# First MLP of a two-layer trunk on Trainium2: its shift and scale loaded by halves of columns, and no unread TensorE products ahead of it

## The reference, cut to what matters

```
sh_m, sc_m, gt_m, sh_f, sc_f, gt_f = split(silu(c) @ ada_w[i] + ada_b[i], 6)
h  = rms_norm(x, norm_g[i, 0]) * (1 + sc_m) + sh_m
x  = x + gt_m * rms_norm(mixer(h), norm_g[i, 1])
hf = rms_norm(x, norm_g[i, 2]) * (1 + sc_f) + sh_f
x  = x + gt_f * rms_norm(square(relu(hf @ ffn_w1[i])) @ ffn_w2[i], norm_g[i, 3])
```

## Time and profile before

| what | value |
|---|---|
| median of 3 runs | 944.35 us (943.44 to 946.1) |
| the profiled execution's own time | 945.35 us |
| its span in the profile | 943.6 us |
| PE busy | 923.8 us, 98% |
| DVE, ACT busy | 635.5 us (67%), 418.4 us (44%) |
| mean granted clock of PE | 0.996 of full |
| DMA moved | 165.63 MB, mean 176 GB/s |

### The profile page before, as it was taken

The page is one execution under the profiler, slowest core; times in us unless marked ns, Lnnn a source line. Parts: engine busy times, 40 slices in busy tenths (PEclk is TensorE's granted clock), DMA queues, the critical chain, the costliest instruction groups (busy, mean ns, idle before and its releaser), DMA issues.

```text
span 943.6 us, 11434 instructions
## 1 busy us (share of the span) xinstructions
PE 923.8 (98%) x4647; PEld 760.5 (81%) x4647; DVE 635.5 (67%) x624; ACT 418.4 (44%) x513; POOL 43.9 (5%) x76
## 2 busy tenths in 40 slices
PE   8889999999999999999999999999999999999997
PEld 6658877888888888889888888898888888888886
DVE  5696299489578866686667545757856964784444
ACT  6554474455246433264222224555634624643422
POOL 3002000010001001000101000000000000000000
PEclk9999999999999999999999999999999999999999
DMA  9999439617834585424656531273871561246201
GB/s 307 316 352 346 160 135 284 250 55 197 288 114 113 163 331 207 129 71 172 210 178 209 196 114 45 82 275 129 231 265 45 156 223 45 90 122 236 89 23 67
DMA packets 89036, 165.63 MB, mean 176 GB/s; under 512 B 4206, under 2 KB 34002, under 8 KB 88984
## 3 DMA queue, kind: packets, MB, share of 16 engines
q1 hardware_dynamic: 83656, 154.20, 47.6%
q0 software_dynamic: 5328, 10.70, 5.5%
HBM read 158.56 MB, written 6.32 MB: 175 GB/s over the span
## 4 chain that ended last, share of the span: by engine, by line
PE 53%; DVE 1%; issue 0%; ACT 0%; DVEq 0%
PE ps L657 18%; PE ps L658 17%; PE ps L659 17%; PE ps L751 1%; DVE y L1552 0%; DVE in_lo L1563 0%; PE ps L686 0%; ACT in_hi L1191 0%; DVE y L1558 0%; DVE xs L1928 0%; DVE y L1515 0%; DVE y L1509 0%; DVEq L136 0%; ACT work L1163 0%; DVE st L1549 0%
## 5 line engine op out<-in xcount | busy, mean ns | idle before, releaser
L657 PE MATMUL ps<-in_hi,w_parts 128*128 128x512 f32 (+1 forms) x784 | 290.0, 370 | 0.9 <-DVE in_lo L1563 0.4
L658 PE MATMUL ps<-in_lo,w_parts 128*128 128x512 f32 (+1 forms) x784 | 288.1, 367 | 0.0
L659 PE MATMUL ps<-in_hi,w_parts 128*128 128x512 f32 (+1 forms) x784 | 288.1, 367 | 0.0
L1389 DVE TENSOR_TENSOR w_parts<-raw,w_parts 128x2048 fp32r<-128x2048 f32 x81 | 185.5, 2291 | 140.2 <-ACT w_parts L1085 140.1
L1085 ACT ACTIVATE w_parts<-raw 128x2048 fp32r<-128x2048 f32 x81 | 154.8, 1911 | 223.7 <-PE ps L659 204.2
L657 PEld LDWEIGHTS ps<-in_hi,w_parts 128*128 128x128 f32 x784 | 147.8, 188 | 29.4 <-issue 3.3
L659 PEld LDWEIGHTS ps<-in_hi,w_parts 128*128 128x128 f32 x784 | 147.8, 188 | 24.4
L658 PEld LDWEIGHTS ps<-in_lo,w_parts 128*128 128x128 f32 x784 | 147.8, 189 | 24.1
L657 PE MATMUL ps<-w_parts,ops_hi 128*128 128x512 f32 x240 | 93.8, 391 | 2.3 <-DVE y L1441 0.9
L658 PE MATMUL ps<-w_parts,ops_hi 128*128 128x512 f32 x240 | 93.4, 389 | 0.0
L657 PE MATMUL ps<-w_parts,mid_hi 128*128 128x512 f32 x192 | 75.0, 391 | 0.0
(11 more groups left out here) (192 smaller groups left out, 1044.8 us busy)
## 6 DMA issues: line engine op xcount, KB each, us to landing
raw<-in_ffn_w_dram SPq DMA_DIRECT2D x58, 1024.0 KB, 5.4
ada_raw<-in_ada_w_dram SPq DMA_DIRECT2D x56, 512.0 KB, 6.2
xs<-in_ffn_w_dram SPq DMA_DIRECT2D x12, 1024.0 KB, 5.6
raw<-in_conv_in_w_dram SPq DMA_DIRECT2D x16, 512.0 KB, 5.2
xs<-in_ffn_w_dram POOLq DMA_DIRECT2D x6, 1024.0 KB, 8.7
raw<-in_ada_w_dram SPq DMA_DIRECT2D x4, 1024.0 KB, 11.0
ada_sum<-in_ada_w_dram SPq DMA_DIRECT2D x4, 1024.0 KB, 12.8
win<-in_ada_w_dram SPq DMA_DIRECT2D x4, 1024.0 KB, 12.1
```

The costliest lines, as they stand in the source:

```text
L657: nc.tensor.matmul(o, hi, b_hi, start=start, stop=False, skip_group_check=on)
L658: nc.tensor.matmul(o, hi, b_lo, start=False, stop=False, skip_group_check=on)
L659: return nc.tensor.matmul(o, lo, b_hi, start=False, stop=stop, skip_group_check=on)
L1389: nc.vector.tensor_tensor(w_lo[:, u % W_SLOTS, :], raw_of(u), w_hi[:, u % W_SLOTS, :].bitcast(F32), ALU.subtract).then_inc(w_lo_ready, 1)
```

## The change

Four things change, all between the mixer's end and the end of unit 4.

1. The eight late pieces are cut another way. A piece is now 256 rows by 512 columns of shift and the same of scale; four pieces make one half of the columns (`SUMS` 8 and 9). Each is loaded by two DMAs of 512 KB with contiguous runs of 2 KB. In `add_up` a late piece is 4 products of 512 columns in place of 8 of 256.
2. `stay_busy(0, 6)` goes, and the four `turn_up` of the late sums become two `turn_late` (4 small products each). ACT's `copy_late` and DVE's `late_columns` handle four chunks at once.
3. All eight transposed parts go through ACT's `copy_first` to `xt`. The order is chunks 0 to 3 for all tokens, then chunks 4 to 7. Scaling, high part and low part are made chunk by chunk over all 512 tokens.
4. Unit 1 is multiplied chunk by chunk over 512 tokens. PE's order is new: transposes 0 and 1, pieces 14 and 15, transposes 2 and 3 and `turn_late(0)` stand ahead of the first product. On ACT and DVE the splits of unit 3 now stand behind the high and low parts of chunks 4 to 7.

```
 PRE = (... + [(GATE_M, c) for c in range(4)]
-       + [(s, c) for c in range(4) for s in (SCALE_F, SHIFT_F)])
+       + [(h, kk) for h in range(2) for kk in range(UK)])
-SUMS = ... + [(PRE_F + 2 * c, PRE_F + 2 * c + 1) for c in range(4)]
+SUMS = ... + [tuple(PRE_F + UK * h + kk for kk in range(UK)) for h in range(2)]
@@ load_pre
+                if i >= PRE_F:
+                    h, kk = PRE[i]
+                    rows = ada_rows(0)[:, 2 * kk:2 * kk + 2, SHIFT_F * D:(SCALE_F + 1) * D].rearrange("p k (s n) -> p k s n", s=2)
+                    for s in range(2):
+                        sp.dma_start(pre_slot(i)[:, :, s, :], rows[:, :, s, half(h)]).then_inc(pre_in[PRE_SLOTS[i]], 16)
@@ add_up
+                if i >= PRE_F:
+                    for j in range(4):
+                        mm = nc.tensor.matmul(ps[32 * j:32 * (j + 1), sums_bank(n), :], silu_wide[:, 1, 2 * PRE[i][1] + j % 2, :], pre_slot(i)[:, j % 2, j // 2, :],
+                                              start=first, stop=last)
+            def turn_late(h):
+                pe.wait_ge(late_picks, 1)
+                pe.wait_ge(ada_row, cols_value(8 + h))
+                for j in range(4):
+                    mm = nc.tensor.matmul(ps[:, sums_bank(8 + h), 2 * j:2 * j + 2], late_row[:, h, j * P:(j + 1) * P], pick_late[:, :], start=True, stop=True)
@@ PE, ahead of ffn(0)
             add_up(PRE_F)
             add_up(PRE_F + 1)
-            stay_busy(0, 6)
-            turn_up(8)
+            turn_first(0)
+            turn_first(1)
+            add_up(PRE_F + 2)
+            add_up(PRE_F + 3)
+            turn_first(2)
+            turn_first(3)
+            turn_late(0)
@@ start_pairs, new (the old one is in the listing above)
+                need_weights(1)
+                chunk(1, 0)
+                turn_first(4)
+                turn_first(5)
+                chunk(1, 1)
+                add_up(PRE_F + 4)
+                turn_first(6)
+                turn_first(7)
+                chunk(1, 2)
+                add_up(PRE_F + 5)
+                chunk(1, 3).then_inc(unit_done, 1)
+                need_weights(2)
+                pe.wait_ge(xt_copied, len(FIRST_TURNED))
+                add_up(PRE_F + 6)
+                second_unit(2)
+                add_up(PRE_F + 7)
+                second_unit(3)
+                turn_late(1)
+                second_unit(0)
+                pe.wait_ge(cols_read, cols_value(9))
+                second_unit(1).then_inc(unit_done, 1)
+                for u in (3, 4):
+                    need_weights(u)
+                    for m in range(4):
+                        for k in range(UK):
+                            if m == 0:
+                                pe.wait_ge(f_lo, UK + k + 1)
+                            last = feat_products(u, k, m, u - 3, UK + k, COLS, ALL, False, k == UK - 1)
+                        last.then_inc(bank_done, 1)
@@ ACT, new order after first_root(0), first_root(1)
             first_root(2)
             first_root(3)
+            copy_first(0) ... copy_first(3)
+            copy_late(0)
+            for n in range(4):
+                first_hi(n)
+            copy_first(4)
+            copy_first(5)
             split_hi(2)
+            copy_first(6)
+            copy_first(7)
+            copy_late(1)
+            for n in range(4, 8):
+                first_hi(n)
             split_hi(3)
@@ DVE, new order after first_norm(0), first_norm(1)
             first_x(3)
             first_norm(2)
             first_norm(3)
+            late_columns(0)
+            first_input(0), (1), first_lo(0), first_input(2), first_lo(1), first_input(3), first_lo(2), (3)
             split_lo(2)
+            late_columns(1)
+            first_input(4), (5), first_lo(4), first_input(6), first_lo(5), first_input(7), first_lo(6), (7)
             split_lo(3)
```

More of the change, by code:

```diff
@@ L282, in pre_slot @@
                     win[:, 0:4, :].rearrange("p a t -> p (a t)"), win[:, 4:8, :].rearrange("p a t -> p (a t)"))[PRE_SLOTS[i]]
-            return slot.rearrange("p (k n) -> p k n", k=NC)
+            return slot.rearrange("p (k s n) -> p k s n", k=2, s=2) if i >= PRE_F else slot.rearrange("p (k n) -> p k n", k=NC)
         def pre_value(i):
-            return 16 * PRE_SLOTS[:i + 1].count(PRE_SLOTS[i])
+            return sum(32 if b >= PRE_F else 16 for b in range(i + 1) if PRE_SLOTS[b] == PRE_SLOTS[i])
         def sums_of(i):
@@ L941, in start_pairs, with chunk @@
             def start_pairs():
[L944 to L950, removed]
-                    return last
[L953 to L960, removed]
+                def chunk(u, k):
+                    pe.wait_ge(f_lo, k + 1)
+                    for m in range(4):
+                        last = feat_products(u, k, m, u - 1, k, COLS, ALL, k == 0, False)
+                    return last
                 def second_unit(m):
-                    need_weights(2)
                     for k in range(UK):
@@ L1807, in first_lo, with late_columns @@
-            def first_lo(i):
-                dve.wait_ge(f_hi, i + 1)
-                part = first_part(*FIRST_MADE[i]) if i < 4 else (slice(None), slice(2 * FIRST_MADE[i], 2 * FIRST_MADE[i] + 2))
-                nc.vector.tensor_tensor(in_lo[part], xt[part], in_hi[part].bitcast(F32), ALU.subtract).then_inc(f_lo, 1)
+            def late_columns(h):
+                at = ps[:, sums_bank(8 + h), 0:2 * UK].rearrange("p (j s) -> p s j", s=2)
+                c = slice(UK * h, UK * (h + 1))
+                dve.wait_ge(ada_turned, 9 + h)
+                for s, (to, v) in enumerate(((SH_F, V_FSHIFT), (TMP_F, V_FSCALE))):
+                    op = nc.vector.tensor_tensor(to[:, c], at[:, s], vec[:, v + UK * h:v + UK * (h + 1)], ALU.add)
+                op.then_inc(cols_read, 1)
+                dve.wait_ge(cols_read, cols_value(8 + h))
+                nc.vector.scalar_tensor_tensor(out=A_F[:, c], in0=TMP_F[:, c], scalar=1.0, in1=vec[:, V_FG + UK * h:V_FG + UK * (h + 1)],
+                                               op0=ALU.add, op1=ALU.mult).then_inc(mod_step, 1)
@@ L1858, in _ @@
             first_norm(1)
-            columns(8)
-            first_input(0)
-            first_lo(0)
             first_x(3)
```

155 lines of the change are left out of this document (57 added, 98 removed).

## The result

The changed kernel takes 957.06 us (median of 4 runs, 954.14 to 958.36) against 944.42 us for the kernel before (4 runs): ratio 1.0128, 95% interval 1.01 to 1.0155. It is 12.6 us slower. The forecast was 954.2 us in a range of 948.5 to 958.5, slower with a chance of 0.91. The profiled execution took 958.36 us, with a span of 956.6.

A forecast was written before the change was run, and what follows sets the result against it. PE was taken to set the end. 75.5 + 23.3 + 1.2 + 8.75 + 21.8 + 1.2 = 131.75 us for the second projection's first product, against 121.95, 9.8 us later: 954.2 us, range 948.5 to 958.5.

The forecast's parts named there:

- The bound: PE sets the end; a later first product of the second projection, at 121.95 us before, moves the end as much.
- Rival 3: After 122 us: later stages take up the delay, no change, 944.4 us; chance 0.04.
- The loads at nothing: Late pieces: 2 KB runs save 3.2 us of transfer, hidden by the chain through x, so costed at nothing.
- Rival 4: Late pieces: loads set the start, so 2 KB runs give up to 3.2 us, 941.1 us; chance 0.04.
- Rival 6: Late pieces: small DMAs are slow, 512 KB taking 3.0 us, so 10.4 us more, 964.6 us; chance 0.02.
- The first product at 75.5 us: Start of unit 1 on PE: needs all four token blocks and a sum of four pieces, so starts at 75.5 us.
- The new form of `add_up`: Late pieces on PE: 4 products of 512 columns take 1.01 us a piece, as 8 of 256 did.
- Rival 2: Late pieces on PE: new `add_up` loses overlap at 2.2 us, 6 us more, 960 us; chance 0.05.
- The wait for unit 3: PE ahead of unit 3: splits behind the late half end 8.75 us after `turn_late(1)`, PE covers 5.45, waits 3.3 us.
- Rival 1: Ahead of unit 3: wait short or hidden, 3.3 us and the second clock loss go, 949.7 us; chance 0.10.
- The clock: PE around unit 1's start and after the wait for unit 3: granted clock falls, 1.2 us each, range 0 to 1.7.
- my own sign: From the first product on `ops_hi` to the end: forecast wrong if this distance shrinks by more than 1 us.

The follow-up runs named there:

- experiment 3: Changed kernel with each late piece loaded by four DMAs of 256 KB in 1 KB runs, not two of 512 KB in 2 KB runs: 955.17 us, 1.0120.
- experiment 5: Changed kernel with real work moved ahead of unit 1: piece 16 before the late turn, transposes 4 and 5 and piece 17 behind it: 949.61 us, 1.0060.
- Experiment 1: Changed kernel with the splits of unit 3 moved ahead of the late row's copy (ACT) and the late columns (DVE): 949.83 us, 1.0064.
- experiment 11: Kernel before with the splits of unit 3 moved behind its last high and low part on ACT and DVE: 943.94 us, 1.0000.
- experiment 2: Changed kernel with unread products back: 6 ahead of the first transposes, 5 ahead of the late turn, 10 behind it: 951.55 us, 1.0085.
- experiment 4: Kernel before with its six unread products, the line `stay_busy(0, 6)`, deleted: 945.91 us, 1.0023.
- the three repairs: Changed kernel with real work moved ahead of unit 1, early splits of unit 3, and six unread products back ahead of the first transposes: 943.13 us, 0.9996.
- kernel 10: Changed kernel with moved real work, early unit 3 splits, six unread products back, and five more unread products in the mixer: 943.5 us, 0.9996.
- kernel 8: Kernel before with five more unread products in the mixer, two and three in two of PE's waits: 943.46 us, 0.9993.

## Why the prediction was right, point by point

**The bound.** PE sets the end: shown. The time behind the first product of the second projection is 820.4 to 821.7 us in all fourteen kernels, whatever came before it. Rival 3 (later stages take up the delay) falls.

**The loads at nothing.** Right, by experiments 3 and 5: no wait on the path is ended by a late piece behind piece 13. Rivals 4 and 6 fall. The rate is 387 GB/s and not the 401 of the weight units, too small a difference to matter.

**The first product at 75.5 us.** It came at 77.01. But `first_x` began at 61.08 and not 59.64 us; in this execution PE ran at about half clock in the mixer from 35.8 to 42.7 us (0.52 in the mean), twice as long as before. Counted from `first_x` the first product is 15.93 us later against my 15.86. That the sum holds to 0.1 us is in part luck: the late turn began 0.4 us earlier than I had it, and from there to the product it took 0.5 us longer, since DVE got the columns 1.06 us after the turn's start and not 0.75. The late turn was released by ACT's copy, the first product by DVE's low part, as told.

**The new form of `add_up`.** From the start of a piece to the next work it is 0.96 to 1.00 us at full clock, where I took 1.01. Rival 2 falls.

**The wait for unit 3.** Forecast 3.3 us, measured 3.29. The mechanism is right, and the exact size is luck: from the late turn's end to the last split it took 9.04 us and not 8.75, and PE's cover was longer by as much (5.75 and not 5.45). Experiment 1 removed the wait. Rival 1 falls. That this place was dear only with the late second half I had in the sum, and experiment 11 bears it out.

**The clock.** Two terms of 1.2 us each. The first measured 1.35: 2.69 us of products from 77.01 to 79.7 at half clock. The second was mis-sized. In the profiled execution PE ran for 5.95 us of unit 3 at half clock, 3.0 us lost and not 1.2. But this is one execution. In three other kernels with the same wait of 3.30 us (experiments 2, 3 and 5, in this order below) the low stretch is shorter:

```profile
108.00:114.00 6.00, 5.87 (x19) 4.65 (x20) 2.28 (x2) 1.20 (x2) 0.00 (x0) 0.72 0.75 274
109.00:115.00 6.00, 5.74 (x19) 4.60 (x20) 2.41 (x2) 1.16 (x2) 0.00 (x0) 0.72 0.73 262
104.00:110.00 6.00, 5.89 (x19) 4.69 (x20) 2.26 (x2) 1.21 (x2) 0.00 (x0) 0.72 0.78 271
```

In them units 3 and 4 take 23.4 to 23.5 us, against 24.81 in the changed kernel's profile and my 21.8 + 1.2 = 23.0. So this term costs 1.6 to 1.7 us in three profiles, which is my upper bound, and 3.0 in the fourth. In the profiled execution it is 1.8 of the 3.0 us that the sum lacked up to the second projection, the mixer left aside.

The Trainium skill ("TensorE: Matmul & The Clock Gate", Part 1) puts the ramp at under 1% of a typical span. The page says it of a kernel's first matmuls, and I had set it against falls in the middle of one. The size about agrees even so: the mean granted clock of the two profiles is 0.988 and 0.996, 0.8 points apart. But the whole change is 1.28%, and experiments 2 and 4, which touch unread products alone, measure 0.43% and 0.23%. For comparing two versions the term must stay.

**What the sum lacked on the other side.** The new order of unit 3 gives back 1.2 us later. I had written that later work hangs on units 3 and 4 as before, and missed that banks done one by one feed ACT earlier. I had also written that I am wrong if the time behind the first product on `ops_hi` shrinks by more than 1 us. It shrank by 1.2 (821.66 to 820.47): by my own sign this step failed, though it is small beside the loss and of the other direction.

**The balance** of the profiled execution: 956.6 - 953.4 = 3.2 us above my span. It is 1.44 (mixer) + 0.07 (start) + 1.09 (from the first product to the end of the wait for unit 3) + 1.81 (units 3 and 4, clock) - 1.2 (later stages). Of the 1.09, 0.15 is clock, 0.3 the longer late half, and the rest is spread over products, transposes and pieces. The 1.44 is no part of the change. So the errors are of both signs. The median, 957.06 us, lies inside the stated range and at the upper edge of the 951 to 957 that I gave the forecast alone.

**Open.** How much of 12.6 us is clock in the mean over executions is only bracketed. The changed kernel's own times spread over 4.2 us, and I did not separate where. Nor is it separated what the order by chunks and halves costs by itself once the three repairs are in: 0.8 us of the middle part against the kernel before, 1.4 between kernels 10 and 8.

## What to carry to other kernels

When a change makes the first product wait for more data, look first for real work that can be moved into the wait, and only then for filler: here pieces and transposes that stood behind the first product were worth 4.4 us in front of it by the profiles, and 6.4 by the ratios. On engines with a hand-written order, ask for each split or copy what it now stands behind; two lines cost 6 us. A faster transfer is worth nothing until a wait on the path is ended by a DMA.

## What the runs showed of the hardware that I had not expected

After a 3.29 us wait PE ran at half clock for 5.95 us of dense 128x512 products, 0.43 us from one to the next (111.95 to 112.37 in the timeline) against 0.227 at full clock. In three other executions the same wait was followed by a low stretch of only about 3.5 us, as in the kernel before at 37.2 us, and not always from the first product on (in experiment 5 its first three ran at full clock). Six small unread products, 2.38 us of PE time in a wait, were worth 2.2 us in the kernel before; in experiment 2 the same six, with 2.27 us of idle behind them, did not keep the clock up for the transposes.
